# A branch moved ahead of the last down products, with the last products and sums in either arm

## The chip, the cores and the metric

One core of one Trainium2 chip. The metric is device time in microseconds, from the launch of the program to its end on that core. The kernel before took 1599.74 us, the median of three runs (1599.58 to 1599.93).

## What is computed

The reference is a model of two blocks on 256 tokens of width 1024, all in float32. The first block has two layers with attention, a state-space mixer, a gated linear mixer, a feed-forward part and a gated residual. The second block has a recurrent mixer and then a mixture of experts, whose end is what matters here:

```python
def hier_moe(h, ...):
    ...   # each of 256 tokens picks 2 of 32 experts, with weights
    def run_block(args):
        toks, wts, e = args
        xb = hf[toks]
        y = (jax.nn.silu(xb @ w_gate[e]) * (xb @ w_up[e])) @ w_down[e]
        return y * wts[:, None].astype(y.dtype)
    ...
    return out.reshape(B, T, D)

h = h + ffn.astype(h.dtype)
return rmsnorm(h, final_g)[:, N_META:]
```

w_gate and w_up are 1024 x 512 for each expert, w_down is 512 x 1024.

## The kernel before, in words

Each engine has an instruction stream of its own, written out by hand, and waits for the others on semaphores. Python loops are unrolled, so the stream of the tensor engine (PE, TensorE) is long: each product of this kernel is two LDWEIGHTS and two MATMUL instructions, as operands are float32; a transpose is one of each.

**Experts.** The 32 experts are taken in 16 pairs (PAIRS). Each expert has 32 slots (SL) for tokens of each half of the 256 tokens. For a pair, TensorE gathers the tokens' rows by a product with a selection matrix (`gather_two`, `gather`), multiplies them by the gate and the up weights (`expand`), transposes the hidden rows (`hidden_turned`) and the weighted picks (`picks_turned`), multiplies the hidden rows by the down weights (`down`, line 1665 is its product) into two banks, one for each half of 512 output columns, and adds the result to the tokens' rows by a product with the turned picks (`sum_half`, line 1630, called by `sum_up`). VectorE (DVE) copies half 0 of the down result out of its bank (`rows_back`, line 3282), ScalarE (ACT) copies half 1 for the last two pairs (line 2069). Each copy raises `y_ready0` or `y_ready1`.

**Passes.** 32 slots hold all tokens of an expert nearly always. Where one expert is picked more often, a second pass over all pairs is made, and a third, and so on. The number of passes is worked out on the chip from the picks (`count_passes`), written to `passes`, and loaded by each engine into a register (`value_load`). TensorE, VectorE, ScalarE and SyncE then have an `If(n_passes > 1)` around two nested loops (`Fori`) that hold the general path: all 16 pairs again, with addresses in registers. With the inputs timed here there is one pass, so each engine branches over it. On TensorE the skipped body is one gather (16 products), the gate and up products (32), four transposes of the hidden rows and one of the picks, one sum (4 products) and the down products (32), with their waits and the loops' own operations.

**The end.** The weights of the last two pairs come in pieces on SyncE's queue (lines 681 to 692), each with a semaphore (`late_down{k}`, `last_down{k}`), and the final gain behind them (line 695). TensorE runs the down products of pair 14 k by k (four k, eight products each), with the transposes of pair 15 between them. Then, lines 1741 to 1753: wait for the last hidden rows and pick weights; down products of pair 15 for k = 0; the sums of pair 14 (`sum_up`); down products for k = 1 to 3. Then comes the If (line 1766), over which it branches; then, lines 1770 to 1774, waits for `pickT_ready` and `y_ready0` and `y_ready1` against n_passes x 16, and the last four products, the sums of pair 15. Each raises `sum_done`.

On ScalarE the copy of half 1 of pair 14 and of pair 15 come first, then the load of n_passes (line 2071), the If (line 2072), and the squares for the final norm (line 2081), which wait for `sum_done`. On VectorE half 0 of pair 14 and of pair 15 are copied (lines 3315 and 3316), then comes its If (line 3317), and then the products with the final gain (line 3334). SyncE's If stands at line 698, behind all loads.

Of the kernel before, what the change touches and what calls it, by code (L numbers as in the profile page):

```python
# [19 lines left out]
ACT = mybir.ActivationFunctionType  # L20
# [33 lines left out]
KE = DE // P  # L54
# [4 lines left out]
PAIRS = NE // 2  # L59
# [155 lines left out]
def program(nc, d, out):  # L215
# [15 lines left out]
    with ExitStack() as ctx:  # L231
# [5 lines left out]
        def sem(name):  # L237
            if name not in sems:
                sems[name] = ctx.enter_context(nc.semaphore(name))
            return sems[name]  # L240
# [164 lines left out]
        yE = c.take(D)  # L405
# [10 lines left out]
        last_hidT = mflat[:, 1024:1536].rearrange("p (k n) -> p k n", k=KE)  # L416
        late_pickT = mflat[:, 1536:1536 + P]
# [13 lines left out]
        moe_bank = [psum[(i + N_TILES - 2) % NPS] for i in range(NPS)]  # L431
# [347 lines left out]
        def _(pe):  # L779
# [95 lines left out]
            b = claim(TILE["cp"])  # L875
# [20 lines left out]
            for layer in range(DEPTH):  # L896
                T = lambda name: TILE[name, layer]
                if layer == 0:
# [5 lines left out]
                    b = claim(TILE["factor"])  # L904
# [5 lines left out]
                if layer == 0:  # L910
                    pe.wait_ge(sem("rows_loaded"), 16 * 16)
                    for i, (src, r) in enumerate(((prow1, DEPTH * ROWS1), (prow2, 80))):
                        tile = TILE["cp_rest"] + i
                        b = claim(tile)
# [4 lines left out]
                b = claim(T("lr"))  # L919
# [3 lines left out]
                for k in range(KD):  # L923
                    q = 32 * (k % 4)
                    ins = mm(b[q:q + 24, 0:SEQ], w[:, k, :], xT[:, k, NM:NTOK], start=(k < 4), stop=(k >= 4), skip_group_check=True)
# [27 lines left out]
                b = claim(T("dt"))  # L953
                for t in range(NT):
                    ins = mm(b[:, 8 * t:8 * t + 8], lrT[:, P * t:P * t + P], dt_rows[:, :], start=True, stop=True)
                ins.then_inc(psum_full(T("dt")), 1)
                b = claim(T("gk"))
# [4 lines left out]
                for j in range(2):  # L962
                    ins = mm(b[:, 256 * j:256 * j + 256], gw2[:, layer, P * j:P * j + P], lrT[:, :], start=True, stop=True)
# [9 lines left out]
                for i in range(3):  # L973
                    tile = T("xbT") + i
                    b = claim(tile)
                    for j in range(4 if i < 2 else 2):
                        src = cx[:, j, P * i:P * i + P] if i < 2 else cx[:, 4 + j, 0:P]
                        ins = nc.tensor.transpose(b[:, P * j:P * j + P], src, ident[:, :])
# [3 lines left out]
                b = claim(T("keT"))  # L982
                for t in range(NT):
                    for j in range(2):
                        o = P * (2 * t + j)
                        ins = nc.tensor.transpose(b[:, o:o + P], ke[:, j, P * t:P * t + P], ident[:, :])
# [4 lines left out]
                b = claim(T("cumc"))  # L991
                dA = s8[:, 2:4, 0:8]
                for t in range(NT):
                    mm(b[:, 16 * t:16 * t + 8], tri[:, :], dA[:, t, :], start=True, stop=True)
                    ins = mm(b[:, 16 * t + 8:16 * t + 16], ones[:, :], dA[:, t, :], start=True, stop=True)
                ins.then_inc(psum_full(T("cumc")), 1)
                for t in range(NT):
                    for q in range(2):
                        tile = T("cumb") + 2 * t + q
                        b = claim(tile)  # L1000
                        for j in range(4):
                            hh = 4 * q + j
                            ins = mm(b[:, P * j:P * j + P], dA[:, t, hh:hh + 1].to_broadcast([P, P]), tri[:, :], start=True, stop=True)
                        ins.then_inc(psum_full(tile), 1)
                b = claim(T("cb"))
                for t in range(NT):
                    for gg in range(2):
                        o = P * (2 * t + gg)
                        ins = mm(b[:, o:o + P], cx[:, 4 + gg, P * t:P * t + P], cx[:, 6 + gg, P * t:P * t + P], start=True, stop=True)
# [4 lines left out]
                b = [claim(T("gst") + half) for half in range(2)]  # L1014
                for cc in range(3):
                    t, half = cc // 2, cc % 2
                    lo = GLA_C * half
                    for j in range(2):
                        for par in range(2):
                            o = GLA_DK * par  # L1020
                            v0 = 2048 + P * (2 * j + par)
                            ins = mm(b[half][o:o + GLA_DK, 256 * t + P * j:256 * t + P * j + P], keT[lo:lo + GLA_C, t, j, o:o + GLA_DK],
                                     tm[lo:lo + GLA_C, t, v0:v0 + P], start=True, stop=True)
                    if cc:
                        ins.then_inc(psum_full(T("gst") + half), 1)
                b = [claim(T("gat")), claim(T("gat") + 1)]
                for t in range(NT):
                    for j in range(2):
                        o = P * (2 * t + j)
                        for par in range(2):  # L1030
                            lo = 64 * par
                            ins = mm(b[par][:, o:o + P], ki[lo:lo + 64, j, P * t:P * t + P], qd[lo:lo + 64, j, P * t:P * t + P], start=True, stop=True)
# [25 lines left out]
                for t in range(NT):  # L1058
                    b = claim(T("yd") + t)
                    for hh in range(SSD_H):  # L1060
                        ins = mm(b[:, 64 * hh:64 * hh + 64], decay[:, t, hh, :], xdt[:, t, 64 * hh:64 * hh + 64], start=True, stop=True)
                    ins.then_inc(psum_full(T("yd") + t), 1)
                b = claim(T("st"))
# [10 lines left out]
                b = [claim(T("go") + par) for par in range(2)]  # L1074
# [142 lines left out]
                def down(j, name, first, last):  # L1217

                    pairs = 2 if j < DOWN_CHUNKS - 1 else KF // 2 - 2 * j
                    return seven(T("dn"), name, hid_blocks(2 * j, pairs), lambda s_: hsum[:, j % 2, s_], down_blocks(ch + j, pairs),  # L1220
                                 lambda s_: wsum[:, (FFN_CHUNKS + j) % 2, s_, 0:512 * pairs].rearrange("p (a n) -> p a n", a=pairs), first, last)
# [403 lines left out]
            def sum_half(half, first, weights=pickT):  # L1625

                sums = []
                for t in range(NT):
                    r = 2 * SL * t
                    sums.append(mm(moe_bank[4 + 2 * t + half][:, :], weights[r:r + 2 * SL, :], yE[r:r + 2 * SL, 512 * half:512 * half + 512],  # L1630
                                   start=first, stop=True, skip_group_check=True))
                return sums
# [7 lines left out]
            def sum_up(n, first, weights=pickT):  # L1640

                for half in range(2):
                    pe.wait_ge(sem(f"y_ready{half}"), n + 1)
                pe.wait_ge(sem("pickT_ready"), n + 1)
                for half in range(2):
                    sum_half(half, first, weights)
# [93 lines left out]
                    picks_turned(PAIRS - 1, P)  # L1740
            pe.wait_ge(sem("hidT_ready"), PAIRS)
            pe.wait_ge(sem("pickT_ready"), PAIRS)
            for k in range(KE):
                for half in range(2):
                    if half == 0 or k == KE - 1:
                        pe.wait_ge(sem(f"last_down{k + half}"), 32)
                    ins = down(PAIRS - 1, w_last, half, k, last_hidT, 0)
                    if k == KE - 1:
                        ins.then_inc(sem("y_full"), 1)
                if k == 0:  # L1750
                    sum_up(PAIRS - 2, False, late_pickT)

            def pair(n):

# [9 lines left out]
                rows_down(n)  # L1764

            with pe.If(n_passes > 1):
                with pe.Fori(1, n_passes) as turn:
                    with pe.Fori(0, PAIRS) as i:
                        pair(turn * PAIRS + i)
            pe.wait_ge(sem("pickT_ready"), n_passes * PAIRS)  # L1770
            for half in range(2):
                pe.wait_ge(sem(f"y_ready{half}"), n_passes * PAIRS)
                for ins in sum_half(half, False):
                    ins.then_inc(sem("sum_done"), 1)

        @block.scalar
        def _(act):
# [280 lines left out]
            def pair(n, turn0):  # L2058

                act.wait_ge(sem("gate_full"), n + 1)  # L2060
                if not turn0 or n:
                    act.wait_ge(sem("hid_ready"), n)
                act.activation(silE, moe_bank[0][:, :], ACT.Silu).then_inc(sem("sil_ready"), 1)  # L2063

            for i in range(PAIRS):
                pair(i, True)
            for i in (PAIRS - 2, PAIRS - 1):
                act.wait_ge(sem("y_full"), 2 * i + 2)
                act.activation(yE[:, 512:1024], moe_bank[3 if i < PAIRS - 1 else 1][:, :], ACT.Copy).then_inc(sem("y_ready1"), 1)
            act.wait_ge(sem("passes_ready"), 1)  # L2070
            n_passes = act.value_load(passes[0:1, 0:1], min_val=1, max_val=MAX_PASSES)
            with act.If(n_passes > 1):
                with act.Fori(1, n_passes) as turn:
                    with act.Fori(0, PAIRS) as i:
                        pair(turn * PAIRS + i, False)
            for i in range(2 * NT):
                t, half = i % 2, i // 2
                act.wait_ge(sem("sum_done"), i + 1)
                if t:
                    act.wait_ge(sem("rows_gained"), i)  # L2080
                act.activation(squares[i], moe_bank[4 + 2 * t + half][:, :], ACT.Square, scale=D ** -0.5,
                               accum_out=st1[:, 40 + i:41 + i]).then_inc(sem("squares_done"), 1)
# [8 lines left out]
        def _(v):  # L2091
# [1186 lines left out]
            def rows_back(n, halves=range(2), first_bank=2):  # L3278

                for half in halves:  # L3280
                    v.wait_ge(sem("y_full"), n * 2 + half + 1)
                    nc.vector.tensor_copy(yE[:, 512 * half:512 * half + 512], moe_bank[first_bank + half][:, :]).then_inc(sem(f"y_ready{half}"), 1)  # L3282
# [30 lines left out]
            pick_weights(PAIRS - 1, PAIRS - 1, PAIRS - 1)  # L3313
            picks_back(PAIRS - 1, o=P)
            rows_back(PAIRS - 2, (0,))
            rows_back(PAIRS - 1, (0,), 0)
            with v.If(n_passes > 1):
                with v.Fori(1, n_passes) as turn:
                    TS(rank, rank, float(SL), None, ALU.subtract).then_inc(sem("rank_shifted"), 1)
                    with v.Fori(0, PAIRS) as i:  # L3320
                        n_ = turn * PAIRS + i
                        v.wait_ge(sem("rank_shifted"), turn + 1)
                        pick_rows(i, 2, n_ * 2)
                        pick_weights(i, n_, n_)
                        rows_in(n_)
                        hidden(n_)
                        hidden_back(n_)
                        picks_back(n_)
                        rows_back(n_)

            def gained(t, half):

# [53 lines left out]
```

## Time and profile before

| | |
|---|---|
| median of 3 runs | 1599.74 us |
| the profiled execution, its own time | 1599.36 us |
| its span, first to last instruction | 1597.3 us |
| TensorE busy | 1570.2 us, 98% |
| VectorE, ScalarE, GpSimd busy | 56%, 12%, 2% |
| read from memory | 372.28 MB, 234 GB/s over the span |

The profile is one execution. A busy share counts instructions that the engine itself works on; waits, branches, register operations and the issuing of transfers are done by the engine's sequencer and are shown with a q (PEldq is TensorE's). The sequencer runs ahead of its engine, so that a branch can begin while earlier products still run. PE is TensorE's MATMULs, PEld its LDWEIGHTS. L1665 is line 1665 of the kernel. "<-" behind an idle time names what ended it; "issue" is time in which the engine waited for nothing that the profile shows.

### The profile page before, as it was taken

To read this page: it belongs to the slowest core of one execution; us is meant where nothing else is said; L and a number is where in the kernel's file an instruction comes from. 1 tells how busy PE (TensorE), PEld (TensorE's weight loads), DVE (VectorE), ACT (ScalarE), POOL (GpSimd) and SP (SyncE) were. 2 spreads that over 40 slices of the span, in tenths; PEclk is the share of its full clock that TensorE was granted. 3 is DMA by queue.
4 is the path that set the end of the run, shared out by engine and by line. 5 is a ranking of instruction groups with operands and counts; after the bars stand their busy time and mean duration, and the time that the engine had idled before them with its cause. 6 is when DMAs were issued, how large, how long until landed. Compare 5 with 4: busy or idle time off the path is not lost.

```text
span 1597.3 us, 20637 instructions
## 1 busy us (share of the span) xinstructions
PE 1570.2 (98%) x8777; PEld 998.8 (63%) x8777; DVE 896.0 (56%) x1549; ACT 192.5 (12%) x311; POOL 36.0 (2%) x60
## 2 busy tenths in 40 slices
PE   8999999999999999999999999999999999999997
PEld 4866499974458564999744876899533333333332
DVE  5896766764659876676646676795432223121122
ACT  1321000000114110000001331410000000000001
POOL 1001000000010010000000000000000000000000
PEclk9999999999999999999999999999999999999999
DMA  6532545562534326355426333446999999999997
GB/s 213 204 106 105 181 145 164 169 216 105 212 103 162 106 105 217 114 167 184 178 105 247 122 106 132 158 173 262 376 411 426 425 424 428 426 425 427 428 421 302
DMA packets 129780, 374.68 MB, mean 235 GB/s; under 512 B 17220, under 2 KB 65672, under 8 KB 116888
## 3 DMA queue, kind: packets, MB, share of 16 engines
q1 hardware_dynamic: 118864, 370.62, 60.9%
q10 hardware_dynamic: 10824, 2.72, 0.7%
q8 instruction: 71, 1.16, 0.3%
q14 instruction: 21, 0.17, 0.0%
HBM read 372.28 MB, written 1.05 MB: 234 GB/s over the span
## 4 chain that ended last, share of the span: by engine, by line
PE 87%; DMA 10%; DVE 1%; SPq 1%; issue 0%; ACT 0%; POOL 0%; POOLq 0%; DVEq 0%
PE bank L870 16%; PE bank L1182 16%; PE bank L801 10%; PE bank L1619 10%; PE bank L813 6%; PE bank L1665 5%; PE bank L1435 4%; PE bank L1385 3%; DMA h<-in_w_down 3%; DMA turned_rows<-in_w_down 3%; DMA turned_rows<-in_w_gate 2%; PE bank L1307 2%; PE bank L1165 2%; PE bank L1468 2%; PE bank L1317 2%; PE bank L821 2%
## 5 line engine op out<-in xcount | busy, mean ns | idle before, releaser
L801 PE MATMUL bank<-weights,turned_rows 128*128 128x512 f32 x384 | 169.3, 597 | 0.4 <-DVE turned_rows L2118 0.4
L3265 DVE TENSOR_TENSOR bc<-mix,bank 128x512 f32<-128x512 f32 x16 | 17.3, 1079 | 216.1 <-PE bank L1619 216.1
L870 PE MATMUL bank<-arena 128*128 128x512 f32 x296 | 133.2, 592 | 0.0
L801 PEld LDWEIGHTS bank<-weights,turned_rows 128*128 128x128 f32 x384 | 72.5, 192 | 86.3 <-issue 85.8
L1182 PE MATMUL bank<-arena 128*128 128x128 f32 x960 | 110.5, 275 | 0.0
L1182 PEld LDWEIGHTS bank<-arena 128*128 128x128 f32 x960 | 108.8, 192 | 0.0
L870 PEld LDWEIGHTS bank<-arena 128*128 128x128 f32 x296 | 56.0, 190 | 69.9 <-issue 67.9
L813 PE MATMUL bank<-turned_rows,weights 128*128 128x256 f32 x448 | 98.6, 380 | 0.0
L813 PEld LDWEIGHTS bank<-turned_rows,weights 128*128 128x128 f32 x448 | 84.6, 190 | 12.1 <-issue 0.7
L1619 PE MATMUL bank<-arena,rows_late 128*64 128x512 f32 x248 | 88.8, 595 | 1.0 <-DMA weights<-in_w_up 0.6
L1665 PE MATMUL bank<-arena,mix 128*32 128x512 f32 x480 | 79.6, 594 | 2.4 <-DMA weights<-in_w_down 1.5
L870 PE MATMUL bank<-weights,arena 128*128 128x512 f32 x172 | 78.8, 593 | 0.0
L1619 PE MATMUL bank<-arena,mix 128*64 128x512 f32 x264 | 74.5, 595 | 2.7 <-DMA arena<-in_w_up 1.8
L3282 DVE COPY arena<-bank 128x512 f32<-128x512 f32 x30 | 20.8, 692 | 96.3 <-PE bank L1665 96.3
L1182 PE MATMUL bank<-turned_rows,weights 128*128 128x128 f32 x640 | 74.7, 275 | 0.0
L1182 PEld LDWEIGHTS bank<-turned_rows,weights 128*128 128x128 f32 x640 | 73.1, 192 | 0.0
L1782 ACT ACTIVATE arena<-bank 128x512 f32<-128x512 f32 (+1 forms) x68 | 38.2, 578 | 264.6 <-PE bank L801 141.0
L2191 DVE TENSOR_TENSOR arena<-weights 128x1024 f32<-128x1024 f32 (+1 forms) x22 | 25.9, 1176 | 77.2 <-PE bank L870 61.0
L745 POOL TENSOR_TENSOR st<-st,mhalf 128x1 f32<-128x1 f32 (+3 forms) x26 | 30.9, 1187 | 1552.0 <-DVE st L2223 517.6
L1665 PE MATMUL bank<-weights,mix 128*32 128x512 f32 x288 | 56.7, 593 | 3.1 <-DMA h<-in_w_down 1.4
L870 PEld LDWEIGHTS bank<-weights,arena 128*128 128x128 f32 x172 | 32.5, 190 | 40.2 <-issue 40.2
L2063 ACT ACTIVATE mix<-bank 128x512 f32<-128x512 f32 x16 | 9.6, 597 | 391.0 <-PE bank L1619 391.0
(540 smaller groups left out, 2553.8 us busy)
## 6 DMA issues: line engine op xcount, KB each, us to landing
weights<-in_w_in SPq DMA_DIRECT2D x28, 2048.0 KB, 8.1
arena<-in_w_gate SPq DMA_DIRECT2D x13, 2048.0 KB, 23.7
arena<-in_w_up SPq DMA_DIRECT2D x12, 2048.0 KB, 35.3
weights<-in_w_ffn_gate SPq DMA_DIRECT2D x22, 1024.0 KB, 5.4
weights<-in_w_ffn_up SPq DMA_DIRECT2D x22, 1024.0 KB, 8.3
weights<-in_w_ffn_down SPq DMA_DIRECT2D x10, 2048.0 KB, 7.9
arena<-in_w_down SPq DMA_DIRECT2D x10, 2048.0 KB, 30.8
weights<-in_w_up SPq DMA_DIRECT2D x9, 2048.0 KB, 20.8
```

Of the source, the lines that this page charges most:

```text
L801: ins = mm(b[:, :], xT[:, k, t0 + P * t:t0 + P * t + P], w[:, k, :], start=(k == 0), stop=(k == KD - 1))
L813: ins = mm(b[:, o:o + nt], w[:, k, P * m:P * m + P], xT[:, k, n0:n0 + nt], start=(k == 0), stop=(k == KD - 1))
L821: ins = nc.tensor.transpose(b[:, q * j:q * j + q], src[0:q, at:at + P], ident[0:q, 0:q])
L870: ins = mm(b[:, :], lhs[:, j, :], rhs[:, j, :], start=(first and j == 0), stop=(last and j == pairs - 1))
L1165: ins = mm(b[:, o:o + P], w[:, k, P * f:P * f + P], xT[:, k, NM + P * t:NM + P * t + P], start=(k == 0), stop=(k == KD - 1))
L1182: ins = mm(b[:, o + P * q:o + P * q + P], lhs[:, q, k, :], rhs[:, k, :], start=(k == 0), stop=(k == 3))
L1307: ins = mm(b[:, 0:NTOK], slot(c_, KD, 512)[:, k, P * m:P * m + P], xT[:, k, 0:NTOK], start=(k == 0), stop=(k == KD - 1))
L1385: ins = mm(b[:, 256 * m:256 * m + 256], slot(uc, KD, 512)[:, k, P * (2 * (u % 2) + m):P * (2 * (u % 2) + m) + P], xT[:, k, NM:NTOK], start ...
L1435: ins = mm(b[:, o + P * m:o + P * m + P], lhs[:, m, k, :], rhs[:, k, :], start=(k == 0), stop=(k == 3))
L1619: ins = mm(moe_bank[bank][TILE_COLS * e:TILE_COLS * e + TILE_COLS, :], xs[:, k, o + TILE_COLS * e:o + TILE_COLS * e + TILE_COLS], w[e](k), ...
L1665: ins = mm(moe_bank[first_bank + half][at:at + SL, :], rows[:, k, src:src + SL], w[e](2 * k + half), start=(k == 0), stop=(k == KE - 1), s ...
L1782: act.activation(dst, src, func, **kw).then_inc(psum_free(tile), 1)
```

## The change

The down products of the last pair, with the sums of the pair before among them, become a function `last_down`, and the last sums a function `last_sums(pairs)`. The If now comes ahead of both, behind the waits for the last hidden rows and pick weights. Its first arm holds `last_down`, the general path, and `last_sums(n_passes * PAIRS)`; an Else arm, which is new, holds `last_down` and `last_sums(PAIRS)`, whose waits are against constants. Both arms are written out in the stream, the first ahead of the second. With one pass the branch goes over the first arm. ScalarE loads the count ahead of both of its copies, makes the first, branches, and has the second in either arm. VectorE branches ahead of its copy of half 0 of the last pair, which stands in either arm. SyncE and GpSimd are as before.

```diff
             pe.wait_ge(sem("hidT_ready"), PAIRS)
             pe.wait_ge(sem("pickT_ready"), PAIRS)
-            for k in range(KE):
+
+            def last_down():
+
+                for k in range(KE):
+                    for half in range(2):
+                        if half == 0 or k == KE - 1:
+                            pe.wait_ge(sem(f"last_down{k + half}"), 32)
+                        ins = down(PAIRS - 1, w_last, half, k, last_hidT, 0)
+                        if k == KE - 1:
+                            ins.then_inc(sem("y_full"), 1)
+                    if k == 0:
+                        sum_up(PAIRS - 2, False, late_pickT)
+
+            def last_sums(pairs):
+
+                pe.wait_ge(sem("pickT_ready"), pairs)
                 for half in range(2):
-                    if half == 0 or k == KE - 1:
-                        pe.wait_ge(sem(f"last_down{k + half}"), 32)
-                    ins = down(PAIRS - 1, w_last, half, k, last_hidT, 0)
-                    if k == KE - 1:
-                        ins.then_inc(sem("y_full"), 1)
-                if k == 0:
-                    sum_up(PAIRS - 2, False, late_pickT)
+                    pe.wait_ge(sem(f"y_ready{half}"), pairs)
+                    for ins in sum_half(half, False):
+                        ins.then_inc(sem("sum_done"), 1)
...
             with pe.If(n_passes > 1):
+                last_down()
                 with pe.Fori(1, n_passes) as turn:
                     with pe.Fori(0, PAIRS) as i:
                         pair(turn * PAIRS + i)
-            pe.wait_ge(sem("pickT_ready"), n_passes * PAIRS)
-            for half in range(2):
-                pe.wait_ge(sem(f"y_ready{half}"), n_passes * PAIRS)
-                for ins in sum_half(half, False):
-                    ins.then_inc(sem("sum_done"), 1)
+                last_sums(n_passes * PAIRS)
+            with pe.Else():
+                last_down()
+                last_sums(PAIRS)
...
-            for i in (PAIRS - 2, PAIRS - 1):
+
+            def second_half_back(i, b):
+
                 act.wait_ge(sem("y_full"), 2 * i + 2)
-                act.activation(yE[:, 512:1024], moe_bank[3 if i < PAIRS - 1 else 1][:, :], ACT.Copy).then_inc(sem("y_ready1"), 1)
+                act.activation(yE[:, 512:1024], moe_bank[b][:, :], ACT.Copy).then_inc(sem("y_ready1"), 1)
+
             act.wait_ge(sem("passes_ready"), 1)
             n_passes = act.value_load(passes[0:1, 0:1], min_val=1, max_val=MAX_PASSES)
+            second_half_back(PAIRS - 2, 3)
             with act.If(n_passes > 1):
+                second_half_back(PAIRS - 1, 1)
                 with act.Fori(1, n_passes) as turn:
                     with act.Fori(0, PAIRS) as i:
                         pair(turn * PAIRS + i, False)
+            with act.Else():
+                second_half_back(PAIRS - 1, 1)
...
             rows_back(PAIRS - 2, (0,))
-            rows_back(PAIRS - 1, (0,), 0)
             with v.If(n_passes > 1):
+                rows_back(PAIRS - 1, (0,), 0)
...
+            with v.Else():
+                rows_back(PAIRS - 1, (0,), 0)
```

## Rows read from the trace of the kernel before

**Rows 1.** Page, busy time of each engine (share of the span), number of instructions.
```profile
PE 1570.2 (98%) x8777; PEld 998.8 (63%) x8777; DVE 896.0 (56%) x1549; ACT 192.5 (12%) x311; POOL 36.0 (2%) x60
```

**Rows 2.** Chain that ended last, 1560 to 1600 us: start, us, what.
```profile
1562.31 15.82 DMA weights<-in_w_down
...
1578.27 1.92 PE bank L1665 x16
1580.19 1.92 PE bank L1630 x8
1582.11 5.29 PE bank L1665 x48
1587.40 0.43 issue
1587.83 2.01 PE bank L1630 x8
```

**Rows 3.** Timeline of TensorE, VectorE, ScalarE, 1570 to 1590 us: start, us, instruction.
```profile
1575.62 1.92 PE L1665 MATMUL bank<-arena,mix 128*32 128x512 f32 x16
1578.27 0.62 PE L1665 MATMUL bank<-arena,mix 128*32 128x512 f32 x2 [0.73 <-DMA weights<-in_w_down]
...
1575.64 0.29 DVE L3276 COPY bc<-bank 128x128 f32<-128x128 f32 x1 [0.50 <-PE bank L1658]
...
1586.61 0.69 DVE L3282 COPY arena<-bank 128x512 f32<-128x512 f32 x1 [9.17 <-PE bank L1665]
1589.08 1.30 DVE L3334 TENSOR_TENSOR xn<-bank,weights 128x512 f32<-128x512 f32 x2 [1.77 <-PE bank L1630]
...
1587.47 0.60 ACT L2069 ACTIVATE arena<-bank 128x512 f32<-128x512 f32 x1 [9.26 <-PE bank L1665]
1588.96 0.60 ACT L2081 ACTIVATE mix<-bank 128x512 f32<-128x512 f32 x1 [0.90 <-PE bank L1630]
```

**Rows 4.** The lines of three of the four If: queue, duration ns min/median/max, start.
```profile
L1766 PEldq COMPARE_BRANCH  x1: 1663/1663/1663, 1585.9 to 1585.9; - x1
...
L3317 DVEq COMPARE_BRANCH  x1: 72/72/72, 1586.6 to 1586.6; - x1
...
L2072 ACTq COMPARE_BRANCH  x1: 58/58/58, 1588.2 to 1588.2; - x1
```

**Rows 5.** Page, DMA queues: packets, MB, share of 16 engines.
```profile
q8 instruction: 71, 1.16, 0.3%
```

**Rows 6.** Windows between code packets: us, busy (instructions) by engine, clock, DMA share.
```profile
690.01:703.94 13.93, 13.93 (x127) 13.93 (x126) 9.48 (x17) 0.90 (x2) 0.00 (x0) 1.00 0.49 152
703.94:722.49 18.55, 18.55 (x168) 18.55 (x167) 15.88 (x23) 1.80 (x4) 0.55 (x1) 1.00 0.64 204
722.49:735.71 13.22, 13.22 (x121) 13.22 (x120) 8.54 (x14) 0.90 (x2) 0.00 (x0) 1.00 0.58 181
...
1585.04:1588.23 3.19, 2.76 (x26) 0.85 (x20) 0.69 (x1) 0.60 (x1) 0.00 (x0) 1.00 0.14 58
```

**Rows 7.** DMA view of 1585.0 to 1585.1, then of 1587.5 to 1589.4 in 40 slices.
```profile
q8 instruction: 1, 0.02, 63.4%
...
GB/s 0 0 0 0 0 0 0 0 0 0 0 0 0 0 0 345 0 0 0 0 0 0 0 0 0 0 0 0 0 0 0 0 0 0 0 0 0 0 0 0
...
q8 instruction: 1, 0.02, 3.3%
```

**Rows 8.** Windows of 1575 to 1583 us, columns as before.
```profile
1575.00:1577.00 2.00, 1.98 (x21) 0.55 (x17) 0.67 (x3) 0.00 (x0) 0.00 (x0) 1.00 1.01 404
...
1579.00:1581.00 2.00, 2.00 (x16) 0.65 (x10) 0.00 (x0) 0.00 (x0) 0.00 (x0) 1.00 1.03 398
1581.00:1583.00 2.00, 2.00 (x18) 0.55 (x18) 0.00 (x0) 0.00 (x0) 0.00 (x0) 1.00 0.87 340
```

**Rows 9.** Windows behind TensorE's last product, columns as before.
```profile
1590.00:1593.30 3.30, 0.00 (x0) 0.00 (x0) 2.45 (x7) 2.96 (x8) 1.10 (x2) 1.00 0.00 0
1593.30:1597.30 4.00, 0.00 (x0) 0.00 (x0) 0.34 (x1) 0.13 (x1) 0.00 (x0) 0.50 0.70 262
```

## The prediction

> **What bounds the kernel now.** TensorE is busy for 98% of the span [rows 1], so what counts is which engine ends the last stretch. The chain of waits of the last 40 us answers that [rows 2]: until 1578.14 the chain is a transfer of expert weights, and from 1578.27 it is TensorE alone: the first quarter of the last pair's down products, the sums of the pair before it, the other 48 MATMULs, 0.43 us of "issue", the last sums. From 1578.27 on no weight is late, so every microsecond that TensorE loses there moves the end. The timeline shows the three engines of the change [rows 3]: TensorE ended pair 14's products at 1575.62 + 1.92 = 1577.54 and waited 0.73 us for weights; VectorE sat idle for 9.17 us ahead of its last half copy, ScalarE for 9.26 us ahead of its own. Whatever they do there costs nothing.
>
> The "issue" of 0.43 us is what the change can take away. By the instructions of the line of each If, TensorE's branch begins at 1585.9 (its sequencer runs ahead of the products) and takes 1663 ns, where the same branch takes 72 and 58 ns on VectorE and ScalarE [rows 4]. It ends at 1585.90 + 1.66 = 1587.56, then come a register operation and a wait, and the sums start at 1587.83. So what matters is why one branch takes 1.66 us.
>
> **Code is fetched in blocks.** Queue 8 carries only instructions: 71 packets, 1.16 MB, so 16 KB each [rows 5]; from one to the next TensorE starts 127 + 126 = 253 MATMULs and LDWEIGHTS where the packets meet idle transfer engines (the windows of [rows 6] begin and end at a packet, each found in the DMA view by narrowing it); 8,777 of each over 70 gaps make 251, and waits come on top. So a block is 256 instructions and each turn into a new block calls for one more. The last two packets: the 70th falls into 1585.0 to 1585.1; it took 63.4% of 16 x 0.1 us = 1.01 us and had landed by 1586.05. The 71st stands in the 16th slice of 1587.5 to 1589.4, at about 1588.23 [rows 7], 0.67 us after the branch had ended and only 26 + 20 = 46 instructions behind the 70th [rows 6]. I read it so: the branch went into the next block, whose packet was the 70th; it could go on 1.51 us after that packet's end; and on arriving it asked for the block after, whose packet began 0.67 us later, with nothing else on the engines.
>
> **Where the branch stands and where it goes.** One k of the last down products is 8 products and 16 MATMULs [rows 2], so a product is two MATMULs and two LDWEIGHTS. The block turn behind the 70th packet came at least 0.67 us ahead of it (1584.4) and hardly before 1582.1, when TensorE had just gone on; at 8 instructions in 0.43 us (48 MATMULs and as many LDWEIGHTS in 5.29 us) the branch is 28 to 75 instructions into its block. It skips the general path: 84 products x 4, 5 transposes x 2 and some 25 waits and loop operations, about 370. It lands at 400 to 445, in the next block (256 to 511), as read above.
>
> With the change the branch is taken 146 instructions earlier (36 products x 4, two waits): at 140 to 185 of the block before. It now skips the first arm: the 146, the 370 and some 20 of the last sums, about 536. It lands at 676 to 721, **two blocks on** (512 to 767), which nothing has asked for. And the second arm (146 + 18) crosses once more, into a third block, after 47 to 92 instructions, about where k = 1 begins.
>
> **What the change costs and saves, part by part.**
> 1. *TensorE, between the last product and the last sums.* The branch, the register operation and the wait on a product of registers go. Bounds: nothing saved, and all of the 0.43 us. VectorE's half is ready in time (copy 1586.61 to 1587.30); ScalarE's copy ends at 1588.07 [rows 3], and the sums of the second half, some 0.9 us behind the first, would start at about 1588.3. I take −0.4 us.
> 2. *TensorE, the branch ahead of the products.* It waits first for the last pick weights (copied at 1575.64 + 0.29 = 1575.93 [rows 3]) and runs ahead of the 16 MATMULs that started at 1575.62 [rows 3]: it begins at about 1576.0. Its cover is the transfer that ended the wait at 1578.14: 2.1 us. No row shows a branch to a block that isn't there, so I bound it. Least: 58 to 72 ns, as on the other engines, or 1.66 us, as here before; both are covered and cost 0. With a fetch: 0.67 us to the packet, 1.0 us of packet, 1.51 us to the end of the branch, in sum 3.2 us even with idle transfer engines. They aren't idle: their share is 1.01 and 1.03 until 1581 and 0.87 in the 2 us after [rows 8]. What that does to a code packet is seen at 722 us: after a quiet packet the next comes 168 + 167 = 335 instructions later instead of 256 (79 at 18 per us = 4.4 us late), the one after that 241 later (64 too many in all, 3.6 us late) [rows 6]. I take 3.0 us, less than either, as the queue runs dry within it (bounds 0 and 5). So: 1576.0 + 0.67 + 3.0 + 1.05 + 1.51 = 1582.2, against 1578.14 before: **+4.1 us** (bounds 0 and 6).
> 3. *The second crossing.* The third block is asked for at 1582.2. The 70th packet, asked for in the same stretch, began 2 to 3 us after its turn; so 1584.9, landed 1585.9, usable 1587.4. TensorE needs it after k = 0 and the sums of the pair before, 3.8 us [rows 2] plus 0.4: 1586.5. **+0.9 us** (bounds 0 and 1.7: nothing if the first stall is longer or a sequential turn doesn't have the 1.51 us).
> 4. *ScalarE and VectorE.* ScalarE's wait, its load of the count, two register operations and the branch move between its two copies, VectorE's branch ahead of its last copy. Cover: the 9.26 and 9.17 us of idle time [rows 3], that hold even a branch of 1.66 us. Behind the last copy they had 0.9 us of wait for the sums [rows 3], so nothing is gained either. 0. Queued behind ScalarE's new early wait is only its copy of half 1 of the pair before; TensorE loads the same count behind its first pair, so it is there long before.
> 5. *DMAs.* None is issued, moved or waited for otherwise; SyncE and GpSimd keep their programs. 0.
>
> Sum: −0.4 + 4.1 + 0.9 = +4.6 us. The profiled execution took 1599.36 us (span 1597.3), so it would take 1603.96; the median of the three runs stands 0.38 us above it, so 1604.3. About 0.2% (3.2 us) is what a measurement of this kernel can tell from no change.
>
> The Trainium skill ("Runtime: NRT & Kernel Launch", section "Instruction fetch mechanics") says that a taken branch whose target is outside the current window of two pages forces a fetch by DMA before execution goes on. This speaks against the change: by it the sum is +4.6 us, without it −0.4 us. The branch of 1.66 us with a packet behind it [rows 4, 7] agrees as far as it goes; no row here shows such a miss, and the page gives no duration for one.
>
> **The rivals.**
> *All is resident, not slower* (0.22). If TensorE keeps several blocks beyond the next, the target is there. Then the 1663 ns was something else, and there is one candidate: the branch ended 0.16 us after the last product's end (1587.40), so it may wait until TensorE is empty. The late products end at 1577.54, the branch at 1577.7, still under the cover to 1578.14; no crossing stalls. Only the −0.4 is left: 1599.3. Against it: the other engines' branches don't wait for their engine (VectorE's was over in 72 ns under a copy of 692 ns), and the 71st packet came right behind the branch. The decision lies at 2.1 us of branch: below, it gains. The same section of the skill says that TensorE's instruction memory is 128 KiB, 2048 instructions; by that alone the target would be inside.
> *A fetch without the 1.51 us* (0.09). If the block is usable when its packet ends, the branch ends at 1580.7: +2.6, no second stall, −0.4: 1601.9. For it: the 1.51 us rests on one branch.
> *The clock falls* (0.12). TensorE would be idle from 1577.54 to about 1582.2, 4.7 us. The granted clock was 1.00 up to 1593.3 and 0.50 (1.2 instead of 2.4 GHz) after it, where TensorE had done nothing since 1589.84 [rows 2, 9], so 3.5 us later. If it falls, the 3.8 us of k = 0 and the sums take up to 7.6, which swallows the second stall: +3.8 − 0.9, up to 1607.2.
> *Faster by over 0.2%* (0.02): nothing in the end stretch that the change touches holds 3.2 us.
> The forecast has the rest, 0.55, with a range of its own from 1601.5 to 1607.0.
>
> **Numbers.** Of the forecast's 0.55 about a fifth lies below 1602.9, since the lateness of the packet may be less than 2 us: slower 0.44 + 0.12 = 0.56; within 0.2%: 0.11 + 0.22 + 0.09 = 0.42; faster 0.02. The range has to take in the resident case at its low end: 1599.2 to 1607.6.
>
> **What would show it.** In the profile of the changed kernel: TensorE's branch at about 1576.0 with 5 to 7 us instead of 1663 ns; a code packet (the 70th) begun between 1577 and 1581, and a 71st 2 to 3 us behind the branch's end; the first product of the last pair at about 1582.2 with its idle time put down to issue, not to a weight transfer; perhaps a gap of about 1 us ahead of k = 1; the last sums following the last product with no 0.43 us; branches of ScalarE and VectorE under 0.1 us each. It is wrong if TensorE's branch takes under 2.1 us: then the first product still starts at 1578.2 and the end comes 0.4 us sooner.

## The result, and the profile after

The changed kernel takes 1606.18 us (median of six runs, 1605.18 to 1607.12) where the kernel before takes 1599.84 (1599.31 to 1600.34): ratio 1.004, interval 1.003 to 1.0051, so 6.3 us slower. The profiled execution took 1605.18 us, its span is 1603.0 us against 1597.3: +5.7 us. The work is the same, and the page says so; only the code queue has one packet more:

```profile
PE 1571.7 (98%) x8777; PEld 999.4 (62%) x8777; DVE 895.8 (56%) x1549; ACT 192.5 (12%) x311; POOL 36.0 (2%) x60
...
q8 instruction: 72, 1.18, 0.3%
```

The chain that ended last, start, us, what, answers to [rows 2]:

```profile
1578.55 4.12 issue
1582.67 3.49 PE bank L1665 x16
1586.16 2.00 PE bank L1630 x8
1588.16 5.29 PE bank L1665 x48
1593.44 0.05 issue
1593.49 2.01 PE bank L1630 x8
```

Read it from the top. The weights for the last pair landed at 1578.55, 0.41 us later than before. That is the scatter of what lies ahead of the change: in the other profiles of this study they landed between 1577.87 and 1580.82. TensorE then did nothing for 4.12 us and waited for nothing that a semaphore shows; before, that gap was 0.14 us. Counted from its own last product, it was idle for 4.71 us, as its timeline says:

```profile
1582.67 0.90 PE L1665 MATMUL bank<-arena,mix 128*32 128x512 f32 x2 [4.71 <-issue]
```

The first quarter of the products and the sums behind it run from 1582.67 to 1588.16, 5.49 us instead of 3.84. The other 48 MATMULs take 5.29 us as before. The gap ahead of the last sums is 0.05 us instead of 0.43, and these take the same 2.01 us.

The rows of the branches on TensorE, VectorE and ScalarE, answering to [rows 4] (duration min/median/max in ns, start):

```profile
L1777 PEldq COMPARE_BRANCH  x1: 6133/6133/6133, 1576.5 to 1576.5; - x1
```
```profile
L3334 DVEq COMPARE_BRANCH  x1: 72/72/72, 1577.2 to 1577.2; - x1
```
```profile
L2087 ACTq COMPARE_BRANCH  x1: 58/58/58, 1578.0 to 1578.0; - x1
```

and the windows around TensorE's, with the columns of [rows 6]: third from the end is its granted clock, second from the end the share of the transfer engines.

```profile
1577.00:1579.00 2.00, 0.96 (x12) 0.05 (x4) 0.69 (x1) 0.60 (x1) 0.00 (x0) 1.00 1.04 411
1579.00:1581.00 2.00, 0.00 (x0) 0.00 (x0) 0.00 (x0) 0.00 (x0) 0.00 (x0) 1.00 1.03 393
1581.00:1583.00 2.00, 0.33 (x4) 0.16 (x8) 0.00 (x0) 0.00 (x0) 0.00 (x0) 0.97 0.90 351
1583.00:1585.00 2.00, 2.00 (x12) 0.44 (x8) 0.00 (x0) 0.00 (x0) 0.00 (x0) 0.50 0.57 220
1585.00:1587.00 2.00, 2.00 (x12) 0.57 (x6) 0.00 (x0) 0.00 (x0) 0.00 (x0) 0.68 0.34 132
1587.00:1589.00 2.00, 2.00 (x18) 0.51 (x18) 0.00 (x0) 0.00 (x0) 0.00 (x0) 1.00 0.00 0
```

The branch on TensorE runs from 1576.48 to 1582.61. In the DMA view of 1580.0 to 1580.1 the code packet begins:

```profile
q8 instruction: 1, 0.02, 64.1%
```

That is 64.1% of 1.6 engine-us, 1.03 us, so it begins at 1580.05, 3.57 us after the branch, and lands at 1581.08; the branch ends 1.53 us later. Almost as soon as TensorE works again, the windows show it at a granted clock of 0.50 (1.2 GHz instead of 2.4), until about 1586.3: they count 12 MATMULs in each 2 us there and 24 from 1589 to 1591, at 1.00.

So the profiled difference is +0.41 (ahead of the change) + 3.98 (4.12 − 0.14 of issue) + 1.65 (5.49 − 3.84, slow clock) − 0.38 (0.43 − 0.05) = +5.66 us, of the 5.7.

### The profile page after: what moved, and what is told of

Its sections match the earlier page's. It is cut to its first block, busy times and chain, and to the rows that moved or that the text cites. A ratio compares the mean times of both kernels' runs of the same rounds, so it can differ in the third digit from the quotient of the medians.

```text
span 1603.0 us, 20636 instructions
## 1 busy us (share of the span) xinstructions
PE 1571.7 (98%) x8777; PEld 999.4 (62%) x8777; DVE 895.8 (56%) x1549; ACT 192.5 (12%) x311; POOL 36.0 (2%) x60
## 3 DMA queue, kind: packets, MB, share of 16 engines
HBM read 372.28 MB, written 1.05 MB: 233 GB/s over the span
## 4 chain that ended last, share of the span: by engine, by line
PE 87%; DMA 9%; DVE 2%; SPq 1%; issue 1%; POOL 0%; ACT 0%; POOLq 0%; DVEq 0%
PE bank L870 16%; PE bank L1182 16%; PE bank L801 10%; PE bank L1619 10%; PE bank L813 6%; PE bank L1665 5%; PE bank L1435 4%; DMA turned_rows<-in_w_down 3%; PE bank L1385 3%; DMA h<-in_w_down 3%; DMA turned_rows<-in_w_gate 2%; PE bank L1307 2%; PE bank L1165 2%; PE bank L1468 2%; PE bank L1317 2%; PE bank L821 2%
```

## The experiments

All on one core, timed beside the kernel before on the same chip. The first time given is the median of the experiment, the second that of the kernel before beside it. The interval given is that of the ratio to it. Not all runs were made on the same chip, so medians of different sets are compared with care; times inside a profile count from the start of its own span.

**TensorE's part undone.** ScalarE's and VectorE's parts stay.

```diff
+            last_down()
             with pe.If(n_passes > 1):
-                last_down()
                 with pe.Fori(1, n_passes) as turn:
...
-                last_sums(n_passes * PAIRS)
-            with pe.Else():
-                last_down()
-                last_sums(PAIRS)
+            last_sums(n_passes * PAIRS)
```

> The changed kernel with TensorE's part undone: its branch stands behind the last products and ahead of the last sums again, ScalarE's and VectorE's parts stay. Theory (all of the cost is TensorE's): as the kernel before within 0.3 us, 1599.8, with 0.43 us of issue ahead of the last sums and a branch of 1.66 us. Rival (ScalarE's or VectorE's branch or the copy behind it costs): over 1 us more than before.

1600.37 us against 1600.12, ratio 0.9999 (0.9989 to 1.0008): as the kernel before. The gap ahead of the last sums is 0.62 us, where I had written 0.43. It also gives the late branch a second time, 0.22 us longer than the 1.66 that I had written:

```profile
L1778 PEldq COMPARE_BRANCH  x1: 1883/1883/1883, 1585.6 to 1585.6; - x1
```

Begun at 1585.60, it ended at 1587.48, 0.35 us after TensorE's last product (1587.13). Its block's packet began at 1584.94 and landed at 1585.96, so the branch ended 1.52 us behind the packet, where the kernel before shows 1.51. It follows the packet, not the end of the products.

**TensorE's part alone.** The other half of the same test.

```diff
-            def second_half_back(i, b):
-
+            for i in (PAIRS - 2, PAIRS - 1):
                 act.wait_ge(sem("y_full"), 2 * i + 2)
-                act.activation(yE[:, 512:1024], moe_bank[b][:, :], ACT.Copy).then_inc(sem("y_ready1"), 1)
-
+                act.activation(yE[:, 512:1024], moe_bank[3 if i < PAIRS - 1 else 1][:, :], ACT.Copy).then_inc(sem("y_ready1"), 1)
             act.wait_ge(sem("passes_ready"), 1)
             n_passes = act.value_load(passes[0:1, 0:1], min_val=1, max_val=MAX_PASSES)
-            second_half_back(PAIRS - 2, 3)
             with act.If(n_passes > 1):
-                second_half_back(PAIRS - 1, 1)
...
-            with act.Else():
-                second_half_back(PAIRS - 1, 1)
...
+            rows_back(PAIRS - 1, (0,), 0)
             with v.If(n_passes > 1):
-                rows_back(PAIRS - 1, (0,), 0)
...
-            with v.Else():
-                rows_back(PAIRS - 1, (0,), 0)
```

> TensorE's part of the change alone: ScalarE and VectorE as in the kernel before, their branches behind their last copies. Theory: as the changed kernel within 0.7 us, 1606.2, with a branch of about 6.1 us on TensorE. A second question: ScalarE's load of the count and its branch now stand between its last copy and the first square again; they end 0.84 us after the copy's start and had 0.9 us of cover, of which the removed 0.43 us would take some: up to 0.1 us more than the changed kernel at most, or nothing.

1606.11 us against 1600.12, ratio 1.0039 (1.0025 to 1.0054), a branch of 6.02 us, 4.13 us of issue. The clock fell here too: k = 0 and the sums took 3.41 + 1.92 = 5.33 us. All of the loss is TensorE's. The 0.1 us of the second question is less than the medians can tell, but the profile shows none of it: from the start of the last sums to the end of the span it is 9.5 us, as in the changed kernel.

**The arm that runs put first.** Nothing else is changed; the branch then falls through instead of being taken.

```diff
-            with pe.If(n_passes > 1):
+            with pe.If(n_passes < 2):
                 last_down()
+                last_sums(PAIRS)
+            with pe.Else():
+                last_down()
                 with pe.Fori(1, n_passes) as turn:
                     with pe.Fori(0, PAIRS) as i:
                         pair(turn * PAIRS + i)
                 last_sums(n_passes * PAIRS)
-            with pe.Else():
-                last_down()
-                last_sums(PAIRS)
```

> The changed kernel with TensorE's two arms in the other order: If(n_passes < 2) holds the last down products and sums, Else the general path, so the arm that runs lies right behind the branch. Theory (the cost is the distance to a block of code that isn't there): the branch isn't taken and ends in under 0.2 us, the first product of the last pair follows the weights within 0.15 us (4.12 us of issue before), the clock stays at 1.00, the sums follow the last product by 0.05 us as in the changed kernel; 0.4 us less than the kernel before (1599.4), some 6.8 us less than the changed kernel. Rival (a branch on TensorE costs by itself, wherever it goes, or it is the early place that costs): within 1 us of the changed kernel's 1606.2.

1600.37 us against 1600.51, ratio 0.9999 (0.999 to 1.0008). The whole loss is gone with the branch in the same early place, so the place alone doesn't cost. Whether it is the taking of the branch or the distance is left to the next experiments, as this branch isn't taken. But the 0.4 us did not show in the median. The rows of the If's line, of this kernel and then of one more take of it:

```profile
L1777 PEldq COMPARE_BRANCH  x2: 86/1814/3542, 1578.5 to 1590.7; - x2
```
```profile
L1777 PEldq COMPARE_BRANCH  x2: 86/1849/3612, 1576.7 to 1588.8; - x2
```

The branch that isn't taken costs 86 ns; the jump from the end of the arm over the general path takes 3.54 us (3.61 in the second take). It begins under the last sums and ends 2.2 us behind them.

**The same, once more,** since the tail of that profile was longer than before.

> The order of arms with the running arm first, once more. In its first profile the sums came 0.05 us behind the last product, but the tail from there to the end was 9.86 us against 9.47 in the kernel before: one store's issue on SyncE took 997 ns where it took 343, while code packets of TensorE's jump over the general path (3.54 us, from the arm's end) were under way. If the jump causes that, this profile shows the same 0.4 to 0.6 us again, and the median is that of the kernel before within 0.3 us; if it was chance, the tail is 9.5 us and the median some 0.4 us below.

1600.63 us against 1599.94, ratio 1.0 (0.9991 to 1.0009). The chain shows the gap closed, and SyncE's timeline where the time went. First the chain:

```profile
1578.92 0.04 issue
1578.96 1.92 PE bank L1665 x16
1580.89 1.92 PE bank L1630 x8
1582.81 5.29 PE bank L1665 x48
1588.09 0.05 issue
1588.14 2.01 PE bank L1630 x8
```

then the stores of the output on SyncE, of this kernel and of the kernel before (duration min/median/max):

```profile
L710 SPq DMA_DIRECT2D out<-xn x2: 352/910/1469, 1593.1 to 1593.8; - x2
```
```profile
L710 SPq DMA_DIRECT2D out<-xn x2: 343/346/348, 1592.8 to 1593.5; - x2
```

The second of the two stores took 1469 ns to issue here and 997 in the first take; it took 343 or 344 in the nine other profiles of this study, none of which has a code packet beside it. In both takes the packet that follows the jump falls beside it (here it begins at 1593.17, the store's issue at 1593.76). The tail from the sums' start to the span's end is 10.3 us here and 9.9 in the first take, instead of 9.5: 0.8 and 0.4 us more, where I had written 0.4 to 0.6. So the 0.4 us gained is given back behind the jump, and here more than that. That the packet delays the issue is likely and not shown: the long issue came twice with the packet and never without, but the first store's issue lies beside the same packet in both takes and took its usual 351 and 352 ns. How the one could delay the other was not tried.

**The general path left out of the first arm.** TensorE's branch is still taken, in the same place, but skips some 170 instructions instead of 536, and nothing is left to jump over at the end of the arm that runs. This leaves out TensorE's further passes, of which these inputs need none.

```diff
             with pe.If(n_passes > 1):
                 last_down()
-                with pe.Fori(1, n_passes) as turn:
-                    with pe.Fori(0, PAIRS) as i:
-                        pair(turn * PAIRS + i)
                 last_sums(n_passes * PAIRS)
```

> The changed kernel without the general path in TensorE's first arm (with one pass it isn't run, but it leaves out the further passes), so the taken branch skips some 170 instructions instead of 536 and lands in the next block of 256, whose packet landed at about 1570.3, 6 us earlier. Theory: no wait for a block, the branch takes under 0.2 us though taken, no idle time of TensorE beyond the weights', 1599.4 us. Rival 1 (a taken branch on TensorE waits until the engine is empty): it ends at about 1578.1 after some 1.6 us; the end is the same, 1599.4, but the row of the branch tells it apart. Rival 2 (the 1.5 us are a fixed price of any entry into another block): 1.5 to 1.7 us, begins at 1576.5 and ends at 1578.1, whatever TensorE does.

```profile
L1777 PEldq COMPARE_BRANCH  x1: 382/382/382, 1576.9 to 1576.9; - x1
```

The two gaps in its chain, ahead of the last pair's products and ahead of the last sums:

```profile
1578.85 0.04 issue
...
1588.03 0.05 issue
```

1599.69 us against 1600.51, ratio 0.9997 (0.9987 to 1.0006). The branch ended at 1577.27, a whole microsecond before TensorE ran out of work (1578.27), so it doesn't wait for an empty engine, and 1.5 us is no fixed price of another block either. Both rivals fall. The block's packet had landed at 1573.57, later than I had written but 3.3 us ahead of the branch. At 382 ns the taken branch is dearer than I expected (under 0.2 us) and far below its cover. Together with the order of the arms this settles the distance: early and taken, the branch costs nothing as long as its block is there. This profile also shows the gain that the change was made for. From the landing of the last weights (1578.85) to the end of the span (1597.57) it is 18.7 us, against 19.2 in the kernel before (1578.14 to 1597.33), with a tail of 9.5 us as before; in the two takes with the jump it is 19.0 and 19.5. The interval of the medians doesn't tell the 0.5 us from nothing.

**The general path twice, in the kernel before.** The late branch then lands two blocks on, with the transfer engines nearly idle. With more than one pass, pairs would be done twice.

```diff
                 with pe.Fori(1, n_passes) as turn:
                     with pe.Fori(0, PAIRS) as i:
                         pair(turn * PAIRS + i)
+                    with pe.Fori(0, PAIRS) as i:
+                        pair(turn * PAIRS + i)
```

> The kernel before with the general path written twice in its place behind the last products (with one pass neither runs; with more, pairs would be done twice), so its late branch skips some 720 instructions and lands two blocks on, at a time when the transfer engines are nearly idle. Theory: 0.7 us to the packet, 1.0 us of packet, 1.5 us to the end of the branch: the branch takes 3.2 to 3.7 us instead of 1.66 and the kernel 1.5 to 2.1 us more, 1601.3 to 1601.9. Rival (a branch on TensorE waits until the engine is empty, and nothing is fetched): 1.66 us as before, 1599.8. Rival 2 (the 4 us of stall in the changed kernel are the block's price even when no weights are moving, and not the lateness of its packet behind them): the branch takes about 6.1 us, 1604.3.

```profile
L1766 PEldq COMPARE_BRANCH  x1: 3524/3524/3524, 1586.6 to 1586.6; - x1
```

1601.91 us against 1600.51, ratio 1.001 (1.0001 to 1.0019). The branch took 3.52 us, in the range of the theory; both rivals (1.66 and 6.1 us) fall: the packet began at 1587.65, 1.04 us after the branch, took 1.05 us, and the branch ended 1.44 us behind it. The gap ahead of the last sums grew from 0.43 to 2.28 us, and the sums from 2.01 to 2.81, for the clock fell behind the gap (windows as above):

```profile
1588.10:1590.40 2.30, 0.04 (x4) 0.02 (x1) 0.00 (x0) 0.60 (x1) 0.00 (x0) 1.00 0.00 0
1590.40:1591.40 1.00, 0.98 (x6) 0.59 (x8) 0.00 (x0) 0.00 (x0) 0.00 (x0) 1.00 0.07 16
1591.50:1593.50 2.00, 1.71 (x6) 0.14 (x2) 1.55 (x3) 1.70 (x5) 0.00 (x0) 0.50 0.00 0
```

**The changed kernel without the last weights' transfers.** The last products then run on what the slots held; place and distance of the branch stay.

```diff
-            for part, (q, pieces) in enumerate(LAST_PARTS):
-                for e in range(2):
-                    ...
-                    sp.dma_start(expert_slot[at][...], ...).then_inc(sem(f"last_down{part}"), 16)
...
-                        if half == 0 or k == KE - 1:
-                            pe.wait_ge(sem(f"last_down{k + half}"), 32)
```

> The changed kernel without the last pair's down weights: SyncE issues none of those ten transfers (4 MB) and TensorE doesn't wait for them, so the last products run with the weights that the slots held before. Place and distance of the branch are those of the changed kernel; only the traffic behind the late pieces is gone. Theory (3 of the branch's 6.1 us are its block's lateness behind the weights): the code packet begins 0.7 to 1.1 us after the branch and the branch takes 3.2 to 3.6 us. Rival (the lateness comes with the early place, or with the two blocks asked for, and not with the weights): 6 us as before. The kernel's time says little, as the end of the products no longer waits for weights: some 1602 by the theory.

```profile
L1770 PEldq COMPARE_BRANCH  x1: 3667/3667/3667, 1576.9 to 1576.9; - x1
```
```profile
1577.00:1579.00 2.00, 1.58 (x16) 0.26 (x8) 0.69 (x1) 0.35 (x1) 0.00 (x0) 1.00 0.05 12
```

With the transfer engines at 0.05 instead of 1.04, the packet began 0.96 us after the branch instead of 3.57, and the branch took 3.67 us (0.1 more than the range of the theory) instead of 6.13. So 2.5 us of the branch are the lateness of its packet behind the weights. The kernel's 1603.01 us (1.0018, 1.0009 to 1.0027) is not to be compared with the others, as work is missing from it. TensorE was idle here for 2.01 us ahead of k = 0, and its clock did not fall.

**Four idle products between the waits and the branch.** Nothing reads their result; they only keep TensorE at work.

```diff
+            for _ in range(4):
+                mm(moe_bank[0][:, :], ident[:, :], xn[:, 0, 0:512], start=True, stop=True, ...)
             with pe.If(n_passes > 1):
```

> The changed kernel with four products more (8 MATMULs of the identity, 16 instructions, into a bank that the last products write anew) between the two waits and TensorE's branch: they keep TensorE at work for some 3.4 us under the fetch. Theory (1.65 us of the loss is the clock at 1.2 GHz): the granted clock stays 1.00, k = 0 and the sums behind it take 3.8 us again instead of 5.5; the branch begins up to 0.9 us later, since the sequencer has to wait for places in the engine's queue, and a second wait of up to 1 us may show ahead of k = 1, where the slow clock had covered it; in all 0 to 1.6 us less than the changed kernel. Rival (the slow start is that of weights or of code, not of the clock): the products of k = 0 are as slow as before.

```profile
1577.26 1.92 PE bank L1665 x16
1579.19 3.63 PE bank L1778 x8
1582.82 0.87 issue
1583.69 1.92 PE bank L1665 x16
1585.61 1.92 PE bank L1630 x8
1587.53 1.41 PE bank L1665 x9
1588.93 0.10 issue
1589.04 4.50 PE bank L1665 x39
1593.53 0.04 issue
```

Here L1778 are the idle products. The branch takes 6.14 us as before, but the idle time is 0.87 us instead of 4.71, the clock stays at 1.00, and k = 0 and the sums take 3.84 us again. Now the second block boundary shows: the 48 MATMULs take 1593.53 − 1587.53 = 6.00 us instead of 5.29, with a gap of its own after nine of them. 1605.25 us against 1600.51, ratio 1.0035 (1.0021 to 1.0048): 4.7 us slower than before, where the changed kernel was 6.3 slower beside other runs. The intervals overlap, so it is the profile that shows it and not the median: from the branch's start to the span's end it is 25.6 us instead of 26.5, that is 1.65 us of clock won and 0.71 of the second boundary lost.

**The changed kernel, once more.**

> The changed kernel beside the others on the same chip: 1606 to 1607 us, a branch of about 6.1 us, and the granted clock at 0.50 for 3.4 us behind it again.

1605.61 us against 1599.94, ratio 1.0031 (1.0019 to 1.0044), a little under the 1606 to 1607 that I had written; a branch of 6.14 us, 4.08 us of issue. The clock was down for 6.8 us in this profile, from 1582.1, not for the 3.4 that I had written: k = 0 and the sums took 3.64 + 2.35 = 5.99 us. How long the clock is down is part of the scatter of this kernel, and the profile of the first measurement, the fastest of its six runs, shows the short case. Why the medians differ by 5.7 to 6.3 us where that profile differs by 5.25 us from the landing of the weights on is not shown further.

## Why the prediction was right, and where a step of it was not

*The direction and the mechanism.* Forecast 1604.3, measured 1606.18, in the range. The range says little, as it was drawn to hold also the case in which nothing is lost; of the 6.3 us of loss the sum had 4.6. The mechanism is what holds. The branch goes into a block of code that isn't there, and TensorE waits for it: shown by the order of the arms (the loss gone), by the distance (gone, with the branch taken in the same place), and by stretching the distance of the late branch (loss made, in the kernel before).

*Part 1, −0.4 us:* the gap went from 0.43 to 0.05, −0.38.

*Part 2, +4.1 us:* +3.98. By its terms: 3.57 us to the packet (0.67 + 3.0 forecast), 1.03 of packet (1.05), 1.53 behind it (1.51). The branch began at 1576.5 instead of 1576.0, and the weights came 0.4 us later as well. That the lateness is the weights' is shown by the run without them: 0.96 us to the packet, so 0.96 + 2.6 rather than 0.67 + 3.0. The 3.0 was set by judgement below the two rows that it leaned on (4.4 and 3.6 us late), with bounds of 0 and 5, so its coming out so near is in part luck. One reading in the placing of the branch is a little off: from 1582.1 to 1585.9 it is about 70 instructions at 8 in 0.43 us, not 75, which moves no block.

*Part 3, +0.9 us:* nothing in the changed kernel, since the slow clock covered it, as the rival said; 0.71 us where the clock was held up. The third block's packet began 3.1 us after the branch's end (2.7 forecast).

*Part 4 and 5, 0:* shown by undoing TensorE's part, and by that part alone. ScalarE's and VectorE's branches took 58 and 72 ns.

*The step that failed* is that the clock stood as a rival with a chance of 0.12 and not in the sum. The sum itself made TensorE idle for 4.7 us, and [rows 9] show the clock down 3.5 us after the last product; the two together made a fall the likeliest case. The later profiles make it likely and no more: in the ten profiles whose clock was still full at TensorE's last product, it fell 2.1 to 5.3 us behind that product. It fell in all three profiles in which TensorE was idle for 4.7 us ahead of k = 0, and cost 1.65 us in one, 2.15 (5.99 − 3.84) in the second and 1.49 (5.33 − 3.84) with TensorE's part alone, within the "up to 3.8" named. With it in the place of part 3 the sum would have been −0.4 + 4.1 + 1.65 = 5.35 us; the medians differ by 6.3 and, in the later runs, by 5.7 and 6.0.

*The rivals.* Residence of the target: refuted by the branch of 6.13 us, whose packet came only after it had begun, and by the one of 3.52 us when the late branch was made to go two blocks on. Its other half, a wait for an empty engine: refuted by the branch of 382 ns under running products and by the one that ended 0.35 us after them. A fetch without the 1.51 us: refuted; each branch of this study that had to wait for its packet ended 1.43 to 1.54 us behind it. The fall of the clock, given 0.12, came true, on top of the forecast's own mechanism and not in its place.

*Open:* what happens in the 1.5 us between the packet's end and the branch's, and why a code packet comes 2.6 us later behind other queues' traffic. Neither was tried by itself.

## What to carry to other kernels

A branch on TensorE with a long unrolled stream cost here what its target's block cost: 86 ns if it falls through, 0.4 us into a block that has landed, 3.5 to 3.7 us into one that nothing has asked for, 6 us when the transfer engines are full. So lay the arm that runs right behind the branch and look at what the jump at its end falls on, keep skipped code short or ahead of a quiet place, and count instructions, not source lines, before a branch is moved or an arm is written out twice. And when a sum makes the tensor engine idle for some microseconds, price the slower clock after it in the same sum.

## What the runs showed of the hardware

- The clock of TensorE fell to 1.2 GHz after a gap of only 2.28 us (with the general path twice): it was granted in full for 1.0 us of new work and then halved. It stayed after a gap of 0.87 us (idle products) and after one of 2.01 us (without the last weights). I had named only the 3.5 us at the end of the kernel. Elsewhere in the same kernels it fell after less. With TensorE's part undone, TensorE waited for weights for 1.41 us at 1484.3, and 0.3 us into its new work the clock was halved for 3.4 us; the kernel before has the same gap, 1.45 us, and kept its clock. In two other profiles (the arm that runs first, and the changed kernel once more) it was down for 3.4 us from about 1153 and 1152, both times with no idle time over 0.3 us in the 5 us before. So the length of one gap doesn't tell whether the clock falls, and such falls are part of the scatter ahead of the change. The windows with TensorE's part undone:

```profile
1484.00:1486.00 2.00, 0.59 (x5) 0.19 (x8) 0.00 (x0) 0.00 (x0) 0.00 (x0) 1.00 1.04 442
1486.05:1489.46 3.41, 3.41 (x20) 1.08 (x16) 0.00 (x0) 0.00 (x0) 0.00 (x0) 0.50 0.99 423
```

- A code packet beside the output's stores went with an issue of 1469 and 997 ns on SyncE instead of 343, in the second of two stores: a jump behind an engine's last work may not be free if it makes that engine fetch.
- A branch that lands in a resident block other than its own took 382 ns on TensorE, one that isn't taken 86.
